# Last neighbourhood group of each layer: low parts of stored rows on GpSimd, gate parts over three steps, output matmuls placed anew

## Chip, cores and metric

One core of one Trainium2 chip. The metric is the device time of one execution in microseconds, lower is better; several executions were timed, and one more was profiled.

## The reference

Two layers of a bidirectional encoder over 1024 positions of width 1024, all in float32, then a last RMS norm:

```python
def hybrid_layer(x, g, w_in, w_out, ...):
    h = rms_norm(x, g)
    z = einsum('bsd,de->bse', h, w_in)
    qd, kd, vd, qn, kn, vn, gate = split(z)
    o_da = diff_attention(qd, kd, vd, lam, lam_init, subln_g)     # 4 heads of 2 x 64, full attention
    o_na = neighbourhood_attention(qn, kn, vn, rpb)               # 8 heads of 64, 8 rows x 16 columns around a position
    o = concatenate([o_da, o_na], axis=-1) * silu(gate)
    return x + einsum('bse,ed->bsd', o, w_out)
```

## The kernel before

Everything is kept transposed: a row block of 128 features by 1024 positions. A float32 product is made of three matmuls in a rounded format (`three`, L930 to L934): high by high, low by high, high by low, where the high part is a rounded copy and the low part the difference to the original. So each operand of a matmul is first copied by ScalarE (ACT; the high part) and then subtracted by VectorE (DVE) or GpSimd (POOL; the low part). A **part** in this text is the three 128x512 matmuls of one k, one of eight row blocks of `h`; a **piece** is the eight parts that give 128 output features for one half (512 positions). The seven first rows of an output piece can be summed early; its last one comes from the last group.

A layer has eight head groups, four of differential attention and four of neighbourhood attention (two heads each). Each runs in steps 1 to 8, one tile of 128 queries a step (`steps`, `step` at L1138): TensorE (PE) makes the scores of the next tile, transposes the probabilities of the last one in blocks of four (`turn_p`), each block copied to `pt_hi` by ACT (L772) and subtracted to `pt_lo` by DVE (L1364), and in even steps weighs the values with a pair of tiles (L1077, L1078) after transposing the reciprocals of the softmax sums (L1088). DVE adds the bias and takes the maximum (L1356), ACT takes the exponential (L797), and `output_pair` (L1410 to L1414) brings a pair into `gate`. Between these blocks, in slots 0 to 3 of `fill`, TensorE does the projection of the group that comes next: V, K, Q and gate pieces, one piece a step, eight parts each. So there is always a step's worth of projection to cover the softmax chain.

The last group of a layer has no next group. Its gate pieces are projected in step 8 of the group before (half 0) and in its own step 1 (half 1), in step 2 there are no parts, and from step 3 on the slots hold parts of the output projection (`LAST_FILL`, `out_piece`). The gated results of the first seven groups wait in DRAM (`mixed_dram`). They are loaded as rows into `h_lo` (L518) as soon as the last piece of `h` has used that row (`row_freed`, counted by the parts of gate half 1), copied to `h_hi` by ACT (`take_mixed`, L831) and subtracted in place by DVE (L1438), at the steps in `TAKEN`. Output parts of pieces 0 and 1 wait for the row of their k (`h_ready`). The weights come in chunks of two pieces: DMA into `w_raw` (L483), high part by ACT (L730), low part by POOL (L577); output chunks 1 to 4 are made at the steps in `LAST_CHUNKS`. POOL also finishes the gate (`silu`, L607 and L609: after ACT's tanh, L757) and spreads the reciprocals (`widen`, L621).

Every engine runs its own queue in the order of the program; the tables say in which step and slot something stands:

```python
    LAST_CHUNKS = {2: 1, 6: 2, 7: 3, 8: 4}
    TAKEN = {2: [0, 1], 3: [2, 3], 4: [4, 5], 5: [6]}
    both = lambda ks: [(t, [k]) for k in ks for t in (0, 1)]
    LAST_FILL = {1: [], 2: [], 3: [[], both([0]), both([1])], 4: [both([2]), [], both([3])],
```

An entry `(p, ks)` stands for the parts `ks` of output piece `p`; the lists of a step are its slots.

Of the kernel before, what the change touches and what calls it, by code (L numbers as in the profile page):

```python
# [26 lines left out]
def hybrid_encoder(nc, x_t, chunks, norm_gain, final_gain, subln_gain, lam_vecs, bias_rows, out_t):  # L27
    D, S = x_t.shape
    NT = D // P
# [31 lines left out]
    LAST_CHUNKS = {2: 1, 6: 2, 7: 3, 8: 4}  # L61
    TAKEN = {2: [0, 1], 3: [2, 3], 4: [4, 5], 5: [6]}
# [131 lines left out]
    with ExitStack() as ctx:  # L194
# [216 lines left out]
        def groups(e, l, attend):  # L411
# [136 lines left out]
        def _(pool):  # L548
# [45 lines left out]

            def mask_edge(l, i):
# [37 lines left out]
            def attend(g, behind):  # L633
                for t, front, ft in steps(g, behind):
                    if front and front.projects(ft) and ft % 2 == 0:
                        w_lo_part(front.chunk(ft) + 1, 1 - front.buffer(ft))
                    if t == 1:
                        silu(g, 0)
                    if front and front.na and t < NT:
                        widen(front, ft)  # L640
                    if t == 1:
                        silu(g, 1)
# [10 lines left out]
                    if not behind and t in LAST_CHUNKS:  # L653
                        out_lo_part(g.l, LAST_CHUNKS[t])
# [39 lines left out]
        def _(act):  # L694
# [144 lines left out]
            def attend(g, behind):  # L839
                for t, front, ft in steps(g, behind):  # L840
# [6 lines left out]
                    if not g.na and t % 2 and t >= 3:  # L847
                        mean_square(g, (t - 3) // 2)
                    for c in range(2):
# [7 lines left out]
                    if front and front.projects(ft) and ft:  # L857
                        piece_part(front, ft)
                    taken = [] if behind else TAKEN.get(t, [])
                    for i in taken[:1]:  # L860
                        take_mixed(g.l, i)
                    if t % 2 == 0:
                        output_half(g, t - 1)
                    if t == NT and behind:
# [4 lines left out]
                        piece_part(behind, 0)  # L869
# [3 lines left out]
                    for i in taken[1:]:  # L873
                        take_mixed(g.l, i)
# [52 lines left out]
        def _(pe):  # L927
# [186 lines left out]
            def step(g, behind, t, front, ft, ended=None):  # L1114
# [8 lines left out]

                def fill(j):
# [3 lines left out]
                    if front and front.projects(ft):  # L1128
# [128 lines left out]
        def _(dve):  # L1257
# [178 lines left out]
            def take_mixed(l, i):  # L1436
                dve.wait_ge(h_hi_done, l * (2 * NT + 1) + NT + i + 1)
# [135 lines left out]
```

## Time and profile before

| what | us |
|---|---|
| median of three runs | 1508.54 |
| the three runs | 1502.69 to 1509.71 |
| the profiled execution | 1503.38 |
| its span | 1501.6 |
| TensorE busy | 1437.1 |
| VectorE busy | 895.6 |
| ScalarE busy | 684.9 |
| GpSimd busy | 459.4 |

The span lies within the execution's own time; all times in rows are counted from the span's start. Layer 0's last group runs from 609.5 to some 690 us, layer 1's from 1340.9 to some 1420 us. Busy time says how long an engine worked, not who waited for whom; for that the rows name the releaser of an idle time in square brackets.

### The profile page before, as it was taken

The numbers are of one execution on the slowest core, as the hardware profiler recorded it, in microseconds if no ns is written. First come the engines' busy times: TensorE is split into PE (matmuls) and PEld (weight loads), VectorE is DVE, ScalarE is ACT, GpSimd is POOL, SyncE is SP. The second block draws the span as 40 slices with busy tenths as digits, with TensorE's granted clock in tenths as the row PEclk, the third lists the DMA queues.
The fourth block names the chain that finished last, engine by engine and source line by source line (L and its number), as shares of the span: only waits on it lengthen the run. The fifth ranks groups of instructions, "written<-read, shape, count | busy, mean of one in ns | idle before, by whom it ended". The sixth has DMA issues, their size and how long they took to land.

```text
span 1501.6 us, 24043 instructions
## 1 busy us (share of the span) xinstructions
PE 1437.1 (96%) x8160; PEld 1170.8 (78%) x8160; DVE 895.6 (60%) x1828; ACT 684.9 (46%) x1306; POOL 459.4 (31%) x370
## 2 busy tenths in 40 slices
PE   7999999999999999899999999999999999997994
PEld 6788787878787888677887878787788888876874
DVE  6666666767655555653436667766666555557323
ACT  5445455544444444542524544544544444445330
POOL 2322223223323232313633132312322323331261
PEclk9999999999999999999999999999999999999997
DMA  4700101021111110301110001010102111121012
GB/s 175 147 29 28 43 21 49 21 60 36 45 51 55 40 59 35 133 15 57 56 47 37 24 35 35 30 40 21 53 22 74 43 52 42 52 96 58 29 56 112
DMA packets 39246, 79.41 MB, mean 53 GB/s; under 512 B 18832, under 2 KB 18832, under 8 KB 39184
## 3 DMA queue, kind: packets, MB, share of 16 engines
q1 hardware_dynamic: 39184, 78.60, 15.7%
q8 instruction: 37, 0.61, 0.2%
q14 instruction: 25, 0.20, 0.0%
HBM read 66.57 MB, written 15.96 MB: 55 GB/s over the span
## 4 chain that ended last, share of the span: by engine, by line
PE 87%; DVE 4%; issue 3%; ACT 2%; SPq 2%; DMA 1%; POOL 0%; DVEq 0%; POOLq 0%; ACTq 0%
PE proj L932 18%; PE proj L934 17%; PE proj L933 17%; PE scores L968 9%; PE turn L1025 5%; PE mix L1077 3%; PE mix L1078 3%; PE mix L1042 2%; PE mix L1041 2%; PE mix L1043 2%; SPq L476 2%; PE scores L1025 2%; DVE prob L1356 1%; PE mix L1051 1%; ACT prob L797 1%
## 5 line engine op out<-in xcount | busy, mean ns | idle before, releaser
L932 PE MATMUL proj<-h_hi,w_hi 128*128 128x512 f32 x1184 | 501.2, 423 | 18.3 <-DVE h_lo L1265 10.1
L934 PE MATMUL proj<-h_hi,w_lo 128*128 128x512 f32 x1184 | 467.3, 395 | 0.0
L933 PE MATMUL proj<-h_lo,w_hi 128*128 128x512 f32 x1184 | 464.3, 392 | 0.0
L932 PEld LDWEIGHTS proj<-h_hi,w_hi 128*128 128x128 f32 x1184 | 223.4, 189 | 82.9 <-issue 36.0
L934 PEld LDWEIGHTS proj<-h_hi,w_lo 128*128 128x128 f32 x1184 | 223.1, 188 | 51.6
L933 PEld LDWEIGHTS proj<-h_lo,w_hi 128*128 128x128 f32 x1184 | 224.5, 190 | 34.3
L1356 DVE CUSTOM_DVE_ANT_0 prob<-scores,inner 128x1024 f32<-128x1024 f32 (+1 forms) x192 | 204.0, 1062 | 72.1 <-PE scores L968 71.4
L577 POOL TENSOR_TENSOR w_lo<-w_raw,w_hi 128x1024 fp32r<-128x1024 f32 x78 | 191.8, 2459 | 179.5 <-ACT w_hi L730 179.4
L1364 DVE TENSOR_TENSOR pt_lo<-turn,pt_hi 128x512 fp32r<-128x512 f32 x208 | 139.2, 669 | 152.5 <-ACT pt_hi L772 151.2
L772 ACT ACTIVATE pt_hi<-turn 128x512 fp32r<-128x512 f32 x208 | 120.5, 579 | 224.4 <-PE turn L1025 223.6
L797 ACT ACTIVATE prob<-prob,nm,escale_now 128x1024 f32<-128x1024 f32 x128 | 158.0, 1235 | 3.3 <-DVE nm L1360 3.2
L1025 PE MATMUL turn<-ident,prob 128*128 128x128 f32 x768 | 116.3, 274 | 16.0 <-DVE pt_lo L1364 11.4
L1025 PEld LDWEIGHTS turn<-ident,prob 128*128 128x128 f32 x768 | 93.3, 140 | 47.4 <-DVE pt_lo L1364 17.3
L621 POOL COPY rrec_wide<-rrec 128x128 f32<-128x128 f32 x64 | 18.6, 291 | 300.1 <-DVE rrec L1389 215.9
L968 PE MATMUL scores<-k_hi,q_hi 64*128 64x512 f32 (+1 forms) x448 | 106.7, 432 | 0.0
L730 ACT ACTIVATE w_hi<-w_raw 128x1024 fp32r<-128x1024 f32 x78 | 82.2, 1054 | 39.0 <-DMA w_raw<-chunks 14.5
L797 ACT ACTIVATE prob<-prob,nm 128x576 f32<-128x576 f32 (+1 forms) x128 | 95.0, 742 | 8.9 <-DVE nm L1360 8.9
L968 PE MATMUL scores<-k_hi,q_lo 64*128 64x512 f32 (+1 forms) x448 | 95.8, 377 | 0.0
L968 PE MATMUL scores<-k_lo,q_hi 64*128 64x512 f32 (+1 forms) x448 | 95.5, 375 | 0.0
L592 POOL TENSOR_TENSOR q_lo<-q_next,q_hi 128x512 fp32r<-128x512 f32 x32 | 41.4, 1293 | 149.6 <-ACT q_hi L762 149.6
L607 POOL TENSOR_SCALAR gate_tanh<-gate_tanh 128x512 f32<-128x512 f32 x32 | 47.8, 1493 | 127.8 <-ACT gate_tanh L757 127.2
L628 POOL TENSOR_TENSOR rms<-msq,power 128x2 f32<-128x2 f32 x32 | 22.6, 705 | 205.0 <-ACT msq L824 205.0
(162 smaller groups left out, 2248.8 us busy)
## 6 DMA issues: line engine op xcount, KB each, us to landing
w_raw<-chunks SPq DMA_DIRECT2D x81, 512.0 KB, 3.2
mixed_dram<-gate SPq DMA_DIRECT2D x28, 256.0 KB, 2.0
edge<-bias_dram SPq DMA_DIRECT2D x32, 224.0 KB, 3.8
h_lo<-mixed_dram SPq DMA_DIRECT2D x14, 512.0 KB, 7.5
xt<-x_t SPq DMA_DIRECT2D x8, 512.0 KB, 9.1
bias_dram<-bias_rows SPq DMA_DIRECT2D x16, 240.0 KB, 5.8
out_t<-prob SPq DMA_DIRECT2D x6, 512.0 KB, 3.0
out_t<-gate SPq DMA_DIRECT2D x2, 512.0 KB, 3.0
```

The costliest lines, as they stand in the source:

```text
L577: pool.tensor_tensor(w_lo[:, b], w_raw[:], f32(w_hi[:, b]), ALU.subtract).then_inc(w_lo_done, 1)
L607: pool.tensor_scalar(gate_tanh[:], gate_tanh[:], 1.0, None, ALU.add).then_inc(gate_plus, 1)
L730: act.activation(w_hi[:, b], w_raw[:], ACT.Copy).then_inc(w_hi_done, 1)
L772: act.activation(dst, src, ACT.Copy).then_inc(turn_hi, 1)
L797: act.activation(s, s, ACT.Exp, bias=nm[:, b, m:m + 1], scale=scale, accum_out=rsum[:, b, m:m + 1]).then_inc(exp_done, 1)
L932: pe.matmul(dst, a_hi, b_hi, start=start, stop=False)
L933: pe.matmul(dst, a_hi, b_lo, start=False, stop=False)
L934: return pe.matmul(dst, a_lo, b_hi, start=False, stop=stop)
L968: return pe.matmul(out, (q_hi, q_lo, q_hi)[p][own, tile], (k_hi, k_hi, k_lo)[p][own, cols], start=p == 0, stop=p == 2)
L1025: last = pe.transpose(dst[:, k * P:(k + 1) * P], prob_of(g.na, t, m, first + k * P, first + (k + 1) * P), ident[:])
L1356: dve.tensor_tensor_reduce(prob_of(g.na, t, m, 0, w), all_scores[:, at:at + w], bias, 1.0, -3e38, ALU.add, ALU.max, mx[:, b, m:m + 1]).the ...
L1364: dve.tensor_tensor(dst, src, f32(hi), ALU.subtract).then_inc(turn_freed, 1)
```

## The change

The low parts of the seven stored rows go from VectorE (`take_mixed`, L1438) to GpSimd (`row_lo`). ScalarE's high parts of these rows stand at new places (`ROWS_HI`: three lists a step, behind the first block of probabilities, ahead of and behind the copy of the mixed pair), GpSimd's in `ROWS_LO`. The sixteen gate parts of the last group, before eight in step 8 of the group before and eight in step 1, become four in that step 8 (`GATE_HEAD`), eight in step 1 and four in step 2 (`GATE_FILL`), and the work on a gate half (scaling, tanh, silu) follows one step later, GpSimd's half 1 in step 3 behind rows 2 and 3. The output parts: steps 3 and 4 as before, step 5 gets two more and step 6 one, steps 7 and 8 two and one fewer; output chunk 1 moves from step 2 to step 4 on ScalarE and GpSimd, there behind rows 4 to 6. The group before the last is written out behind its loop.

```diff
-    LAST_CHUNKS = {2: 1, 6: 2, 7: 3, 8: 4}
-    TAKEN = {2: [0, 1], 3: [2, 3], 4: [4, 5], 5: [6]}
+    LAST_CHUNKS = {4: 1, 6: 2, 7: 3, 8: 4}
+    ROWS_HI = {2: ([0], [1], [2]), 3: ([3], [], []), 4: ([4], [5], [6])}
+    ROWS_LO = {2: [0, 1], 3: [2, 3], 4: [4, 5, 6]}
+    GATE_HEAD = [range(0, 1), range(1, 2), range(2, 4)]
+    GATE_FILL = {1: [[(0, range(4, 6))], [(0, range(6, 8)), (1, range(0, 1))], [(1, range(1, 4))]],
+                 2: [[], [(1, range(4, 6))], [(1, range(6, 8))]]}
...
-                 5: [both([4]), [], both([5])], 6: [both([6]), [(2, range(0, 3))], [(2, range(3, 7))]],
-                 7: [[(3, range(0, 3))], [(3, range(3, 7)), (4, range(0, 2))], [(4, range(2, 7))]],
-                 8: [[(5, range(0, 4))], [(5, range(4, 7))], [(6, most)], [(7, most)]]}
+                 5: [both([4]), both([5]), both([6])],
+                 6: [[(2, range(0, 3))], [(2, range(3, 6))], [(2, range(6, 7)), (3, range(0, 3))]],
+                 7: [[(3, range(3, 6))], [(3, range(6, 7)), (4, range(0, 3))], [(4, range(3, 7)), (5, range(0, 1))]],
+                 8: [[(5, range(1, 4))], [(5, range(4, 7))], [(6, most)], [(7, most)]]}
...
-            with e.Fori(0, NA_G - 1) as i:
+            last = Group(l, True, NA_G - 1, project=False)
+            with e.Fori(0, NA_G - 2) as i:
                 attend(Group(l, True, i), Group(l, True, i + 1))
-            attend(Group(l, True, NA_G - 1, project=False), None)
+            attend(Group(l, True, NA_G - 2), last)
+            attend(last, None)
...
+            def row_lo(l, i):
+                pool.wait_ge(h_hi_done, l * (2 * NT + 1) + NT + i + 1)
+                pool.tensor_tensor(h_lo[:, i, :], f32(h_lo[:, i, :]), f32(h_hi[:, i, :]), ALU.subtract)\
+                    .then_inc(h_ready, 1)
...
-                    if t == 1:
+                    if t == 1 and g.project:
                         silu(g, 0)
+                    for i in ROWS_LO[t] if not behind and t in ROWS_LO else []:
+                        row_lo(g.l, i)
+                    if not behind and t in LAST_CHUNKS:
+                        out_lo_part(g.l, LAST_CHUNKS[t])
                     if front and front.na and t < NT:
                         widen(front, ft)
                     if t == 1:
+                        silu(g, 1 if g.project else 0)
+                    if t == 3 and not g.project:
                         silu(g, 1)
...
                     for c in range(2):
                         p_part(g, t - 1, c)
+                        for i in rows[0] if c == 0 else []:
+                            take_mixed(g.l, i)
                         if front:
                             exponentials(front, ft, c)
...
-            def take_mixed(l, i):
-                dve.wait_ge(h_hi_done, l * (2 * NT + 1) + NT + i + 1)
-                dve.tensor_tensor(h_lo[:, i, :], f32(h_lo[:, i, :]), f32(h_hi[:, i, :]), ALU.subtract)\
-                    .then_inc(h_ready, 1)
```

TensorE's order in step 2 of the last group. `scores` is both the score tile and one of two banks that transposed blocks go to; `turn` is the other. Before:

```order
L968 MATMUL scores<-k_lo,q_hi 128x512 x2
L1025 MATMUL turn<-ident,prob 128x128 x4
L1025 MATMUL scores<-ident,prob 128x128 x4
L1088 MATMUL turn<-ident,rrec_wide 128x128 x2
L1077 MATMUL mix<-pt_hi,v_hl 128x256
```

and of the changed kernel:

```order
L992 MATMUL scores<-k_lo,q_hi 128x512 x2
L1049 MATMUL turn<-ident,prob 128x128 x4
L956 MATMUL proj<-h_hi,w_hi 128x512
L957 MATMUL proj<-h_lo,w_hi 128x512
L958 MATMUL proj<-h_hi,w_lo 128x512
L956 MATMUL proj<-h_hi,w_hi 128x512
L957 MATMUL proj<-h_lo,w_hi 128x512
L958 MATMUL proj<-h_hi,w_lo 128x512
L1049 MATMUL scores<-ident,prob 128x128 x4
```

Two gate parts now stand between the two transposed blocks, and two more behind the second.

GpSimd's queue from the first gate half of the last group to output chunk 1 (`w_lo<-w_raw,w_hi`), before:

```order
L607 TENSOR_SCALAR gate_tanh<-gate_tanh 128x512
L609 TENSOR_TENSOR gate<-gate,gate_tanh 128x512
L621 COPY rrec_wide<-rrec 128x128
L607 TENSOR_SCALAR gate_tanh<-gate_tanh 128x512
L609 TENSOR_TENSOR gate<-gate,gate_tanh 128x512
L621 COPY rrec_wide<-rrec 128x128
L577 TENSOR_TENSOR w_lo<-w_raw,w_hi 128x1024
```

and of the changed kernel:

```order
L621 TENSOR_SCALAR gate_tanh<-gate_tanh 128x512
L623 TENSOR_TENSOR gate<-gate,gate_tanh 128x512
L606 TENSOR_TENSOR h_lo<-h_lo,h_hi 128x1024 x2
L635 COPY rrec_wide<-rrec 128x128
L606 TENSOR_TENSOR h_lo<-h_lo,h_hi 128x1024 x2
L635 COPY rrec_wide<-rrec 128x128
L621 TENSOR_SCALAR gate_tanh<-gate_tanh 128x512
L623 TENSOR_TENSOR gate<-gate,gate_tanh 128x512
L606 TENSOR_TENSOR h_lo<-h_lo,h_hi 128x1024 x3
L586 TENSOR_TENSOR w_lo<-w_raw,w_hi 128x1024
```

Seven subtractions of rows now stand ahead of the chunk, four of them ahead of the second gate half.

ScalarE's queue in steps 2 and 3 (`pt_hi` is a high part of probabilities, `h_hi` of a stored row, `u<-mix` the mixed pair), before:

```order
L772 ACTIVATE pt_hi<-turn 128x4x128
L797 ACTIVATE prob,rsum<-prob,nm 128x512
L772 ACTIVATE pt_hi<-scores 128x4x128
L797 ACTIVATE prob,rsum<-prob,nm 128x512
L831 ACTIVATE h_hi<-h_lo 128x1024
L812 ACTIVATE u<-mix 64x256
L813 ACTIVATE u<-mix 64x256
L730 ACTIVATE w_hi<-w_raw 128x1024
L831 ACTIVATE h_hi<-h_lo 128x1024
```

and of the changed kernel:

```order
L790 ACTIVATE pt_hi<-turn 128x4x128
L849 ACTIVATE h_hi<-h_lo 128x1024
L815 ACTIVATE prob,rsum<-prob,nm 128x512
L790 ACTIVATE pt_hi<-scores 128x4x128
L815 ACTIVATE prob,rsum<-prob,nm 128x512
L775 ACTIVATE gate_tanh<-gate 128x512
L849 ACTIVATE h_hi<-h_lo 128x1024
L830 ACTIVATE u<-mix 64x256
L831 ACTIVATE u<-mix 64x256
L849 ACTIVATE h_hi<-h_lo 128x1024
```

Row 0 now stands between the two blocks of probabilities, rows 1 and 2 around the mixed pair, and chunk 1 has left.

## Rows read from the trace of the kernel before

**Rows 1.** the page's busy time of each engine, us, share of the span, instructions.

```profile
PE 1437.1 (96%) x8160; PEld 1170.8 (78%) x8160; DVE 895.6 (60%) x1828; ACT 684.9 (46%) x1306; POOL 459.4 (31%) x370
```

**Rows 2.** TensorE's losing stretch of both layers, busy us and instructions.

```profile
core 0: us, PE busy (x) PEld busy (x) DVE busy (x) ACT busy (x) POOL busy (x), PEclk, DMA share, GB/s
617.03:654.89 37.86, 28.88 (x166) 22.71 (x165) 29.83 (x64) 21.02 (x39) 6.38 (x8) 0.91 0.21 85
1348.43:1386.61 38.18, 28.89 (x166) 22.49 (x165) 29.84 (x64) 21.30 (x40) 6.38 (x8) 0.91 0.23 90
```

**Rows 3.** TensorE in order of time, layer 0: start us, us, operation [idle before <-releaser].

```profile
598.78 0.50 PE L932 MATMUL proj<-h_hi,w_hi 128*128 128x512 f32 x1
...
609.50 0.50 PE L968 MATMUL scores<-k_hi,q_hi 64*128 64x512 f32 x2
...
610.40 0.50 PE L932 MATMUL proj<-h_hi,w_hi 128*128 128x512 f32 x1
...
617.03 0.51 PE L968 MATMUL scores<-k_hi,q_hi 64*128 64x512 f32 x2
...
617.94 0.66 PE L1025 MATMUL turn<-ident,prob 128*128 128x128 f32 x4
618.43 0.60 PE L1025 MATMUL scores<-ident,prob 128*128 128x128 f32 x4
...
621.70 0.69 PE L1088 MATMUL turn<-ident,rrec_wide 128*128 128x128 f32 x2 [2.67 <-DVE pt_lo L1364]
...
625.61 0.50 PE L968 MATMUL scores<-k_hi,q_hi 64*128 64x512 f32 x2
...
631.19 0.50 PE L932 MATMUL proj<-h_hi,w_hi 128*128 128x512 f32 x1 [2.20 <-DVE h_lo L1438]
...
633.57 0.81 PE L968 MATMUL scores<-k_hi,q_hi 64*128 64x64 f32 x2
...
641.16 0.39 PE L1077 MATMUL mix<-pt_hi,v_hl 128*128 128x256 f32 x1 [0.67 <-DVE pt_lo L1364]
...
643.27 0.51 PE L968 MATMUL scores<-k_hi,q_hi 64*128 64x64 f32 x2
...
649.13 0.44 PE L1021 MATMUL turn<-ident,prob 128*128 128x128 f32 x2 [2.09 <-DVE pt_lo L1364]
...
650.89 0.51 PE L968 MATMUL scores<-k_hi,q_hi 64*128 64x64 f32 x2
...
654.89 0.50 PE L932 MATMUL proj<-h_hi,w_hi 128*128 128x512 f32 x1 [0.49 <-DVE xt L1489]
```

**Rows 4.** the tile h_lo: min/median/max ns, first and last start.

```profile
L831 ACT ACTIVATE h_hi<-h_lo x14: 1041/1048/1062, 622.2 to 1380.4; 128x1024 fp32r<-128x1024 f32 x14
L1438 DVE TENSOR_TENSOR h_lo<-h_lo,h_hi x14: 1218/1224/2593, 623.3 to 1381.5; 128x1024 fp32r<-128x1024 f32 x14
...
DMA to landing us min/median/max: 3.6/7.5/8.9
```

**Rows 5.** VectorE in order of time, layer 0, steps 2 and 3.

```profile
627.40 0.42 DVE L1414 TENSOR_TENSOR gate<-u,gate 128x256 f32<-128x256 f32 x1
628.55 2.59 DVE L1438 TENSOR_TENSOR h_lo<-h_lo,h_hi 128x1024 fp32r<-128x1024 f32 x1 [0.72 <-ACT h_hi L831]
```

**Rows 6.** GpSimd in order of time, layer 0, output chunk 1.

```profile
627.64 2.41 POOL L577 TENSOR_TENSOR w_lo<-w_raw,w_hi 128x1024 fp32r<-128x1024 f32 x1 [4.68 <-ACT w_hi L730]
```

**Rows 7.** groups: line, engine, names, shapes, count | busy us, mean ns | idle before.

```profile
L1364 DVE TENSOR_TENSOR pt_lo<-turn,pt_hi 128x512 fp32r<-128x512 f32 x208 | 139.2, 669 | 152.5 <-ACT pt_hi L772 151.2
...
L772 ACT ACTIVATE pt_hi<-turn 128x512 fp32r<-128x512 f32 x208 | 120.5, 579 | 224.4 <-PE turn L1025 223.6
...
L577 POOL TENSOR_TENSOR w_lo<-w_raw,w_hi 128x1024 fp32r<-128x1024 f32 x78 | 191.8, 2459 | 179.5 <-ACT w_hi L730 179.4
...
L607 POOL TENSOR_SCALAR gate_tanh<-gate_tanh 128x512 f32<-128x512 f32 x32 | 47.8, 1493 | 127.8 <-ACT gate_tanh L757 127.2 <-issue 0.4
L609 POOL TENSOR_TENSOR gate<-gate,gate_tanh 128x512 f32<-128x512 f32 x32 | 41.1, 1286 | 2.7
```

More of the change, by code:

```diff
@@ L652, in attend @@
                         widen(front, ft, g)
-                    if not behind and t in LAST_CHUNKS:
-                        out_lo_part(g.l, LAST_CHUNKS[t])
             def norm_stats(n):
@@ L848, in attend @@
                         mean_square(g, (t - 3) // 2)
+                    rows = ROWS_HI[t] if not behind and t in ROWS_HI else [[]] * 3
                     for c in range(2):
                         p_part(g, t - 1, c)
+                        for i in rows[0] if c == 0 else []:
+                            take_mixed(g.l, i)
                         if front:
@@ L856, in attend @@
                         sum_squared(front, ft)
-                    if front and front.projects(ft) and ft:
+                    if not g.project:
+                        if t in GATE_FILL:
+                            piece_part(g, t - 1)
+                    elif front and front.projects(ft) and ft:
                         piece_part(front, ft)
-                    taken = [] if behind else TAKEN.get(t, [])
-                    for i in taken[:1]:
+                    for i in rows[1]:
                         take_mixed(g.l, i)
@@ L863, in attend @@
                         output_half(g, t - 1)
+                    for i in rows[2]:
+                        take_mixed(g.l, i)
                     if t == NT and behind:
@@ L868, in attend @@
                             mean_square(g, PAIRS - 1)
-                        piece_part(behind, 0)
+                        if behind.project:
+                            piece_part(behind, 0)
                     if not behind:
@@ L872, in attend @@
                             out_hi_part(g.l, LAST_CHUNKS[t])
-                    for i in taken[1:]:
-                        take_mixed(g.l, i)
             def out_hi_part(l, j):
@@ L1122, in step @@
                     sum_pair(g, (t - 3) // 2)
+                if t == NT and behind and not behind.project:
+                    parts = GATE_HEAD
                 def fill(j):
@@ L1127, in fill @@
                             out_piece(g.l, p, ks)
-                    if front and front.projects(ft):
+                    if not g.project:
+                        for p, ks in GATE_FILL[t][j] if t in GATE_FILL else []:
+                            group_piece(g, p, ks)
+                    elif front and front.projects(ft):
                         group_piece(front, ft, parts[j])
@@ L1463, in step @@
                     combine(front, ft)
-                if front and front.projects(ft) and ft:
+                if not g.project:
+                    if t in GATE_FILL:
+                        piece_part(g, t - 1)
+                elif front and front.projects(ft) and ft:
                     piece_part(front, ft)
                 add_pieces(2)
-                taken = [] if behind else TAKEN.get(t, [])
-                for i in taken[:1]:
-                    take_mixed(g.l, i)
                 if g.na and t % 2 == 0:
@@ L1478, in step @@
                         v_part(behind, c)
-                    piece_part(behind, 0)
-                for i in taken[1:]:
-                    take_mixed(g.l, i)
+                    if behind.project:
+                        piece_part(behind, 0)
                 if t == NT and not g.na and behind.na:
@@ L1514, in _ @@
                 from_second(dve, l, step)
+                dve.wait_ge(h_ready, l * HR + NT + NT - 1)
                 for hf in range(2):
```

## The prediction

> **What bounds the kernel now.** I read the page's busy times first, then the stages, then TensorE's rows of the last neighbourhood group, and last the rows of the engines that it waits for. TensorE is busy 96% of the span [rows 1], so only its gaps and slow stretches can be won back. The stage view shows where they are: in the 37.9 us from step 2 of the last group to the first matmul of output piece 2 (layer 0), TensorE is busy 28.9 us and its granted clock is 0.91; the same stretch of layer 1 takes 38.2 us with 28.9 [rows 2]. VectorE is busy 29.8 us there, more than TensorE, GpSimd only 6.4.
>
> [rows 3] give the steps. A score block costs 0.9 us (609.50 to 610.40), a transpose block 0.45 to 0.5 (617.94 to 618.43), the weighing of an outer pair 2.1 (641.16 to 643.27); eight parts (a part is the three matmuls of one k) and two transpose blocks take 6.6 (610.40 to 617.03), so a part is 0.70. Against that, the steps 2 to 5 last 8.6, 8.0, 9.7 and 7.6 us, while their work is 3.9 (0.9 + 2x0.45 + 2.1), 4.6 (0.9 + 0.9 + 4x0.70), 7.0 and 5.1 us: 13.3 us lost per layer, and 0.5 more before 654.89. The gaps named are 2.67, 2.20, 0.67, 2.09 and 0.49 us, all ended by VectorE. Much of the rest is clock: the score matmul at 633.57 lasts 0.81 us, the same one at 643.27 lasts 0.51 [rows 3]; the granted clock of 0.91 says that for about a fifth of the stretch the level was 1.2 GHz in place of 2.4, here 2 us behind the gap of 2.20.
>
> VectorE is late for two reasons. In steps 2 to 5 it makes the low parts of seven stored rows at 1.22 us each and up to two a step, in line with the softmax [rows 4]. And one of them, at 628.55, takes 2.59 us [rows 5]: it starts while GpSimd's subtraction of 627.64 runs [rows 6], and ends 1.1 us after that does, as if it had been held until 630.05.
>
> **What the change does, part by part.** The 56 output parts and 16 gate parts stay; no matmul is added.
>
> *Gate parts.* Four of the sixteen leave step 8 of the group before; step 1 keeps eight; step 2, which has none, gets four. Step 8 shrinks by 4x0.70 = 2.8. Its weighing then needs the last low probability tile earlier, which comes by way of ACT (0.58) and VectorE (0.67) [rows 7]; between no wait and 2.8 I take 1.0, since today's order shows no gap but little room. So step 2 starts 1.8 to 2.0 earlier, at 615.0 instead of 617.03 [rows 3]. Its work is 3.9 + 2.8 = 6.7: the 2.67 us gap is filled.
>
> *Output parts.* Piece 0 and 1 still start in step 3, but are complete at the end of step 5, which gets two parts more (5.1 + 1.4 = 6.5). From the first part of piece 2 on, both kernels have the same 42 output parts left. That gives one mark to compare: today it falls at 654.89 less one transpose block, 654.4.
>
> *Low parts.* Seven leave VectorE, 7x1.22 = 8.5 us per layer. On GpSimd I price one at 2.40 to 2.46, the same subtraction of the same size [rows 6, 7]. The row first: 2.41 against 1.22 us, a factor of two. The Trainium skill (GPSIMD Engine Reference, Engine selection) says the same of two-input elementwise work, and by its table would leave it on VectorE. By its figure alone 7 ops would cost 8.5 us more of engine time; whether that costs anything depends on who waits.
>
> GpSimd's queue from step 1, in layer 0's clock: gate half 0 comes to it about 615.8 and takes 1.49 + 1.29 [rows 7], to 618.7. Row 0 to 621.1. ACT reaches row 1 only behind the second tanh, at about 622.5, so rows 1, 2 and 3 end at 624.9, 627.7 and 630.2 (with a short copy between), gate half 1 at 633.4, rows 4 to 6 at 635.8, 638.2, 640.6 and output chunk 1, moved from step 2 to step 4 and behind them, at 643.0. Stored row 0 is freed at 612.5, and must land before 616.9; the shortest landing is 3.6, the median 7.5 us [rows 4]; the first of the batch should be the short one. At 7.5, ACT's queue is held for some 3 us in step 2, and with it the last tile of that step; at the median it would cost up to 3 us per layer.
>
> *The walk on TensorE.* Step 2: 615.0 + 6.7 + 0.3 wait = 622.0. Step 3: 4.6, and 0.4 since VectorE's gate product (0.42 us, two SBUF inputs like the row of 628.55 [rows 5]) can be held by GpSimd's row 1: 627.0. Step 4: 7.0, and 1.75 because ACT copies row 4 (1.05 [rows 4]) and an exponential ahead of the tile that the weighing needs: 635.75. Step 5: 6.5 and 0.45 for a tile behind that gate product: 642.7. Score block 1.25: piece 2 starts at 643.95, against 654.4. Gain 10.5 per layer. If the gate product of step 4 also loses its place to row 6, VectorE is 2.4 late and piece 2 starts at 646.1: gain 8.3. The middle is 9.4; for a fall of the clock in one layer of three (about 1.3 us each, 3 us of work at half rate) I take off 0.4. So 9 us per layer, 18 in all. Behind the mark I take 0: chunks 2 to 4 keep their steps; piece 4, the first on chunk 2, now starts three parts (2.1 us) earlier within step 7, which bounds a loss there.
>
> *The rest.* One more group body written out of the loop (in each layer the loop runs 2 times, not 3): today's written-out last group loses no time at its start, 609.50 to 617.03; I take 0, with 1 us per layer as the upper end. The wait of VectorE before the last row's low part comes long after the seven: 0.
>
> Profiled execution: 1503.38 - 18 = 1485.4. The three runs shown lie at 1502.69 to 1509.71, the profiled one near their low end; the mean of the four is 1506.1. Against that I give **1488 us**.
>
> **The rivals.**
> (a) *No waits left.* If all 2.8 us of step 8 count and no step waits, piece 2 starts at 640.1: 14.3 per layer, 1477 us. Against it: ACT's order in step 4.
> (b) *The chain stays.* If steps 2 to 5 are long because of score, softmax, exponential, transpose in series and not because of the rows, they keep their 7.6 to 8.6 us, and only the moved parts count: 1.8 + 1.4 = 3.2 per layer, 6.4 in all, about 1499. For it: three of the gaps are ended by the low probability tile, not by a row. Against it: the step just ahead, from 598.78 to 609.50, has the same series and eight parts, and no gap [rows 3].
> (c) *Slower: GpSimd becomes the bound through the shared SBUF port.* From 622.5 on its chain holds seven subtractions and 3.5 us of other work, so chunk 1 is ready at 626 + 7x for a subtraction of x us. At 2.4 that is 642.8, just before it is wanted; at 4.06 it is today's 654.4, and beyond that the kernel is slower. If each subtraction were held by VectorE as VectorE's was, twice its length, 4.8, the mark would be 659.6: 5.2 per layer, 1516 us. For it: the pair at 627.64 and 628.55 shows that one engine holds the other. The Trainium skill (GPSIMD Engine Reference, Key points) says the two share their SBUF interfaces and contend when a VectorE instruction has two SBUF inputs; by it alone this could go either way. Against: in the same pair GpSimd's 2.41 is not stretched, its mean over 78 is 2.46 [rows 7], and VectorE keeps few instructions with two SBUF inputs here once the rows have left.
> (d) *GpSimd late by part of that*, x between 3.5 and 4.06, or the stored rows landing late on top of (b): within 0.5%.
>
> **How the numbers follow.** The walk 0.68, (a) 0.07, (b) 0.14, (c) 0.06, (d) 0.05. The walk's own range is 1480 to 1496: 8.3 to 10.5 per layer, less up to 3 for the landing, over run levels of 1503 to 1509. With (a) below and (b) above, 1478 to 1500 leaves out some 0.15. A measurement here tells about 0.5% from no change, 7.5 us, so 1501 and under is faster: nearly all of the walk, (a), and part of (b), 0.80; same 0.14; slower 0.06.
>
> **What would show it.** Right: piece 2's first matmul at 643 to 647 in layer 0; no gap of 2 us or more in steps 2 to 5; granted clock near 1.0 between the marks; low parts of rows on GpSimd at 2.4 us; one VectorE gate product of 0.42 us stretched by 0.5 to 2.4. Wrong: gaps on TensorE ended by GpSimd's low row or chunk 1 (c); gaps as large as now, ended by the low probability tile (b); ACT idle for DMA in step 2 (late landing); the subtractions on GpSimd well over 2.6 us.

## The result, and the profile of the changed kernel

| | before | changed |
|---|---|---|
| median of four runs, us | 1508.59 | 1486.88 |
| the four runs, us | 1502.69 to 1509.71 | 1484.41 to 1487.66 |
| the profiled execution, us | 1503.38 | 1487.66 |
| its span, us | 1501.6 | 1485.9 |

The ratio of the times is 0.9858 (95% interval 0.9837 to 0.9878): the changed kernel is faster by 1.4%, 21.7 us between the medians and 15.7 between the two profiled executions. The prediction said faster, at 1488.0 us.

First the page's busy times of the changed kernel, to be read against [rows 1]:

```profile
PE 1434.3 (97%) x8160; PEld 1168.9 (79%) x8160; DVE 877.3 (59%) x1814; ACT 684.4 (46%) x1306; POOL 492.0 (33%) x384
```

TensorE runs the same 8160 matmuls in 2.8 us less. VectorE has fourteen instructions fewer, GpSimd fourteen more: the rows of two layers. GpSimd's 32.6 us are 2.33 for each, VectorE's 18.3 are 1.31.

The stage view from step 2 of the last group to the first matmul of output piece 2, in both layers, columns as in [rows 2]:

```profile
core 0: us, PE busy (x) PEld busy (x) DVE busy (x) ACT busy (x) POOL busy (x), PEclk, DMA share, GB/s
616.36:647.23 30.87, 28.89 (x174) 23.37 (x173) 19.32 (x52) 21.12 (x39) 25.70 (x17) 0.94 0.34 128
1339.69:1370.50 30.81, 28.96 (x181) 23.48 (x180) 21.00 (x56) 21.12 (x39) 25.73 (x17) 1.00 0.38 140
```

Here the gain can be seen whole. TensorE is as busy as before, 28.9 us, but in 30.9 us in place of 37.9 and 38.2. (The four gate parts of step 2 now stand in it, 2.8 us; before, about as much went in slow matmuls.) VectorE is down from 29.8 to 19.3 and 21.0, GpSimd up from 6.4 to 25.7, its fullest stretch. The granted clock is 1.00 in layer 1, and 0.94 in layer 0, for a reason that the next rows show: TensorE in order of time, layer 0, columns as in [rows 3].

```profile
616.36 0.50 PE L992 MATMUL scores<-k_hi,q_hi 64*128 64x512 f32 x2
...
621.52 0.38 PE L1101 MATMUL mix<-pt_hi,v_hl 128*128 128x256 f32 x1 [0.18 <-DVE pt_lo L1394]
...
623.62 0.50 PE L992 MATMUL scores<-k_hi,q_hi 64*128 64x512 f32 x2
...
628.32 0.51 PE L992 MATMUL scores<-k_hi,q_hi 64*128 64x64 f32 x2
...
635.58 0.39 PE L1101 MATMUL mix<-pt_hi,v_hl 128*128 128x256 f32 x1 [1.75 <-DVE pt_lo L1394]
...
637.14 0.41 PE L1101 MATMUL mix<-pt_hi,v_hl 128*128 128x256 f32 x1
...
638.55 0.81 PE L992 MATMUL scores<-k_hi,q_hi 64*128 64x64 f32 x2
...
645.88 0.51 PE L992 MATMUL scores<-k_hi,q_hi 64*128 64x64 f32 x2
...
647.23 0.50 PE L956 MATMUL proj<-h_hi,w_hi 128*128 128x512 f32 x1
```

Of the gaps of 2.67, 2.20, 0.67, 2.09 and 0.49 us in [rows 3] only the third stands, the one before the weighing of step 4, and it has grown from 0.67 to 1.75. Behind it, in this layer, the matmuls of the weighing slow from 0.28 to 0.41 us and the next score matmul lasts 0.81: for some 3 us the granted clock was at 1.2 in place of 2.4 GHz.

The rows on ScalarE and GpSimd (the tile `h_lo`, columns as in [rows 4]), and GpSimd's queue in layer 0 in order of time:

```profile
L849 ACT ACTIVATE h_hi<-h_lo x14: 1041/1052/1062, 618.5 to 1361.6; 128x1024 fp32r<-128x1024 f32 x14
L606 POOL TENSOR_TENSOR h_lo<-h_lo,h_hi x14: 2360/2396/2453, 620.3 to 1362.8; 128x1024 fp32r<-128x1024 f32 x14
...
DMA to landing us min/median/max: 3.2/6.9/8.0
```

```profile
620.26 2.39 POOL L606 TENSOR_TENSOR h_lo<-h_lo,h_hi 128x1024 fp32r<-128x1024 f32 x1
623.93 2.40 POOL L606 TENSOR_TENSOR h_lo<-h_lo,h_hi 128x1024 fp32r<-128x1024 f32 x1 [1.28 <-ACT h_hi L849]
...
626.73 4.76 POOL L606 TENSOR_TENSOR h_lo<-h_lo,h_hi 128x1024 fp32r<-128x1024 f32 x2
...
634.49 4.71 POOL L606 TENSOR_TENSOR h_lo<-h_lo,h_hi 128x1024 fp32r<-128x1024 f32 x2
640.59 2.45 POOL L606 TENSOR_TENSOR h_lo<-h_lo,h_hi 128x1024 fp32r<-128x1024 f32 x1 [1.39 <-ACT h_hi L849]
643.00 2.39 POOL L586 TENSOR_TENSOR w_lo<-w_raw,w_hi 128x1024 fp32r<-128x1024 f32 x1
```

No subtraction is stretched: 2.36 to 2.45 us, the price taken from [rows 6, 7]. GpSimd is busy 25.7 of these 30.9 us, but TensorE never waits for it there.

The same 30 us cost VectorE one stretched product. VectorE in order of time, layer 0:

```profile
625.57 1.04 DVE L1444 TENSOR_TENSOR gate<-u,gate 128x256 f32<-128x256 f32 x1
...
640.35 0.42 DVE L1444 TENSOR_TENSOR gate<-u,gate 128x256 f32<-128x256 f32 x1
```

The first starts inside GpSimd's subtraction of row 1 (623.93 + 2.40 = 626.33) and ends 0.28 us after it: it was held. The second starts 0.24 us ahead of row 6 and isn't. Layer 1 has the same pair (1.04 and 0.42).

**Where the 15.7 us come from.** I cut each trace at the first transposes of V of every group, which both kernels have at the same places; us between these marks, the two layers beside each other, and the time in which TensorE sat idle with a named releaser in the 60 us behind the mark of the last group:

| trace | start of the run | groups before step 8 | step 8 | last group and output | idle of that | span |
|---|---|---|---|---|---|---|
| before | 52.8 | 482.2, 480.8 | 73.5, 73.5 | 177.1, 161.7 | 8.9, 9.3 | 1501.6 |
| before, second | 53.9 | 481.5, 481.3 | 73.5, 73.5 | 178.8, 164.0 | 10.5, 10.2 | 1506.4 |
| changed | 53.6 | 482.9, 481.2 | 71.4, 71.3 | 170.8, 154.7 | 1.9, 1.8 | 1485.9 |
| changed, second | 53.3 | 482.2, 481.0 | 71.3, 71.4 | 169.2, 154.5 | 1.9, 1.8 | 1482.9 |
| rows_only | 53.4 | 482.1, 480.9 | 73.5, 73.5 | 177.5, 161.9 | 9.9, 9.8 | 1502.7 |
| rows_chunk4 | 53.1 | 481.0, 480.7 | 73.5, 73.5 | 176.0, 161.7 | 8.7, 8.8 | 1499.3 |
| low_on_dve | 51.9 | 482.0, 481.1 | 71.4, 71.4 | 179.0, 163.1 | 6.5, 6.4 | 1499.8 |
| pool_doubled | 52.5 | 481.5, 481.0 | 71.4, 71.4 | 182.0, 167.2 | 10.7, 8.4 | 1506.9 |
| old_fill | 51.7 | 481.2, 481.0 | 71.4, 71.4 | 171.1, 156.9 | 3.6, 3.9 | 1484.6 |

("Step 8" is the interval between two marks that contains it. The traces come from single executions: low_on_dve's is the slowest of its six, rows_chunk4's the fastest of its twelve.) In the profiled pair, step 8 gives 2.1 in each layer and the last group with the output 6.3 and 7.0: 17.6 us. The start of the run and the six earlier groups of each layer take 1.9 back, and hold nothing that the change touches in substance: over all traces the start scatters from 51.5 to 54.0, the groups from 480.7 to 482.9. Of the 17.6, 14.5 are idle time gone (18.2 less 3.7); the other 3.1 agree with the 2.8 that TensorE's busy time fell by.

### The profile page after: what moved, and what is told of

It is laid out like the page before. It is cut to its first block, busy times and chain, and to the rows that moved or that the text cites. A ratio compares the mean times of both kernels' runs of the same rounds, so it can differ in the third digit from the quotient of the medians.

```text
span 1485.9 us, 23642 instructions
## 1 busy us (share of the span) xinstructions
PE 1434.3 (97%) x8160; PEld 1168.9 (79%) x8160; DVE 877.3 (59%) x1814; ACT 684.4 (46%) x1306; POOL 492.0 (33%) x384
## 4 chain that ended last, share of the span: by engine, by line
PE 89%; DVE 3%; ACT 2%; issue 2%; SPq 2%; DMA 1%; POOL 0%; DVEq 0%; POOLq 0%; ACTq 0%
PE proj L956 19%; PE proj L958 17%; PE proj L957 17%; PE scores L992 10%; PE turn L1049 5%; PE mix L1101 3%; PE mix L1102 3%; PE mix L1066 2%; PE mix L1065 2%; PE mix L1067 2%; PE scores L1049 2%; SPq L485 2%; PE mix L1075 1%; ACT prob L815 1%; DVE pt_lo L1394 1%
## 5 line engine op out<-in xcount | busy, mean ns | idle before, releaser
L1049 PEld LDWEIGHTS turn<-ident,prob 128*128 128x128 f32 x768 | 93.2, 140 | 47.8 <-DVE pt_lo L1394 17.6
L790 ACT ACTIVATE pt_hi<-scores 128x512 fp32r<-128x512 f32 (+1 forms) x80 | 44.1, 552 | 89.2 <-PE scores L1049 89.2
```

What stands on the lines that cost most here:

```text
L790: act.activation(dst, src, ACT.Copy).then_inc(turn_hi, 1)
L1049: last = pe.transpose(dst[:, k * P:(k + 1) * P], prob_of(g.na, t, m, first + k * P, first + (k + 1) * P), ident[:])
```

## The experiments

Each kernel was run beside the kernel before on the same chip; ratios are to it. The kernel before had medians of 1507.49 (17 runs), 1507.51 (27) and 1505.49 (7) us in the three sets, so the 1503.38 of its profiled execution is at the low end.

### The two kernels again

The kernel before, unchanged. Its first runs had lain in two lots, at 1502.7 to 1503.4 and near 1509.

> The kernel before, unchanged, profiled again. Its timed runs lie at two levels, 1502.7 to 1503.4 and 1508.5 to 1509.7 us; the profile shown was one of the lower. If this one is at the higher level, theory A (the extra 5 to 6 us are more stretches of TensorE's clock at its lower level behind the gaps of the last groups) expects the stretch from step 2 to the first part of piece 2 at 40 us or more with a granted clock under 0.91; theory B (they lie elsewhere, in the start, the end or loads) expects that stretch at 37.9 and 38.2 us and a difference in other places.

Measured: 1508.18 us, span 1506.4. The waits of TensorE from 595 to 662 us, and the stage view over the stretches of [rows 2]:

```profile
PE proj L932 <- DVE h_lo L1438: 4.3, 2, 2.3
PE turn L1088 <- DVE pt_lo L1364: 2.7, 1, 2.7
PE turn L1021 <- DVE pt_lo L1364: 2.1, 1, 2.1
```

```profile
617.34:656.85 39.51, 28.93 (x165) 22.86 (x164) 29.82 (x64) 21.01 (x39) 6.38 (x8) 0.91 0.22 84
1350.89:1391.51 40.62, 30.47 (x166) 23.93 (x165) 29.84 (x64) 21.29 (x40) 6.39 (x8) 0.87 0.21 83
```

The same program is 1.7 and 2.4 us longer in the two stretches, and 0.8 us elsewhere (the table). In layer 0 it is the wait for the second row, 2.28 us at 636.82 in place of 0.74; in layer 1 the same wait (0.9 us more idle time in all) and more slow clock, 0.87 (busy 30.5 us in place of 28.9). So most of the difference between these two traces of the kernel before is made in the stretch that the change mends: where gaps and slow clock fall differs from run to run. Theory A held in part: layer 0 came out at 39.5 us and a clock of 0.91, against 40 or more and under 0.91. And there are no two lots: of the 51 executions of the kernel before that were timed beside the experiments, one took 1501.30 us, and the others fill the range from 1503.41 to 1510.43 with no gap of 1 us.

The changed kernel, unchanged:

> The changed kernel, unchanged, timed beside the runs of the kernel before on the same chip: 1485 to 1488 us, ratio 0.984 to 0.988. Theory A (clock) expects its runs closer together than those of the kernel before, since no gap of over 2 us is left.

Measured: 1485.12 us, five runs within 1484.7 to 1485.57, ratio 0.985 (0.9837 to 0.9862), against 1504.11 to 1510.43 for the 17 runs beside it. The last groups have the same gaps as in the first profile (1.9 and 1.8 us), no slow clock behind the 1.75, and are 1.5 us shorter in layer 0. With the gaps of 2 us and more, the scatter has gone.

### One part of the change at a time

**rows_only**: the kernel before, with the low parts of the seven rows on GpSimd at the steps in which VectorE made them. Gate parts, output parts and ScalarE's order stay.

```diff
-                dve.tensor_tensor(h_lo[:, i, :], f32(h_lo[:, i, :]), f32(h_hi[:, i, :]), ALU.subtract)\
+                pool.tensor_tensor(h_lo[:, i, :], f32(h_lo[:, i, :]), f32(h_hi[:, i, :]), ALU.subtract)\
...
+                    for i in taken[:1]:
+                        row_lo(g.l, i)
                     if not behind and t in LAST_CHUNKS:
                         out_lo_part(g.l, LAST_CHUNKS[t])
+                    for i in taken[1:]:
+                        row_lo(g.l, i)
```

> The kernel before with one part of the change: the seven low parts per layer go from VectorE to GpSimd, at the same steps; gate parts, output parts, chunk 1 and ScalarE's order stay. My theory (both parts are needed; the rows are worth about half): in steps 3 to 5 the gaps ended by h_lo on VectorE go, but the row is ready 1.2 us later on GpSimd, and step 2 keeps its gap of some 2.7 us; 4 to 6 us less than before in all, 1500 to 1503. Rival (the rows alone are the cause): 12 us or more less. Rival (GpSimd's twofold length eats it): no gain, TensorE's gaps now ended by POOL h_lo.

Measured: 1504.76 us (12 runs), ratio 0.9989 (0.9978 to 1.0). That is less than the 1500 to 1503 expected, and near the last rival: the part of the change that the profile of before seems to ask for, VectorE's relief, brings 0.1%. TensorE in order of time, layer 0:

```profile
622.16 0.49 PE L1098 MATMUL turn<-ident,rrec_wide 128*128 128x128 f32 x2 [2.67 <-DVE pt_lo L1374]
...
633.09 0.80 PE L942 MATMUL proj<-h_hi,w_hi 128*128 128x512 f32 x1 [3.47 <-POOL h_lo L597]
...
653.93 0.50 PE L942 MATMUL proj<-h_hi,w_hi 128*128 128x512 f32 x1 [1.85 <-POOL h_lo L597]
```

The gap of 2.67 us in step 2 stays to the hundredth: it never was the rows' doing, step 2 had nothing to run. And the waits for rows are now for GpSimd's. Row 1 comes behind chunk 1 in GpSimd's queue:

```profile
628.29 2.43 POOL L577 TENSOR_TENSOR w_lo<-w_raw,w_hi 128x1024 fp32r<-128x1024 f32 x1 [2.14 <-ACT w_hi L740]
630.67 2.36 POOL L597 TENSOR_TENSOR h_lo<-h_lo,h_hi 128x1024 fp32r<-128x1024 f32 x1
```

It is ready at 633.0, and TensorE starts at 633.09, after 3.47 us. So is the queue order the culprit?

**rows_chunk4**: rows_only, with chunk 1 at step 4. It stands behind row 4 there, but ahead of row 5; in the changed kernel it stands behind rows 4 to 6.

```diff
-    LAST_CHUNKS = {2: 1, 6: 2, 7: 3, 8: 4}
+    LAST_CHUNKS = {4: 1, 6: 2, 7: 3, 8: 4}
```

> As rows_only, but with output chunk 1 at step 4 as in the changed kernel, so that GpSimd's row 1 doesn't stand behind it. rows_only gained 2.7 us only; its largest gap, 3.5 us, was ended by POOL h_lo, and that row stood behind chunk 1. If the queue was the cause, that gap goes and the gain is 6 to 9 us (1499 to 1502); the 2.7 us gap of step 2 stays. If the rows on GpSimd are worth nothing by themselves, it stays at 1504 to 1507.

Measured: 1503.79 us (12 runs), ratio 0.9985 (0.9974 to 0.9995), less than expected. The wait of 3.47 us is gone, and three take its place; TensorE, layer 0:

```profile
629.30 0.50 PE L942 MATMUL proj<-h_hi,w_hi 128*128 128x512 f32 x1 [0.99 <-POOL h_lo L597]
633.42 0.50 PE L942 MATMUL proj<-h_hi,w_hi 128*128 128x512 f32 x1 [1.24 <-POOL h_lo L597]
...
647.16 0.50 PE L942 MATMUL proj<-h_hi,w_hi 128*128 128x512 f32 x1 [1.50 <-POOL h_lo L597]
```

The first two are about what a subtraction takes more on GpSimd (2.4 against 1.22 us): row 1 and row 2 are needed as soon as before, and come later. The third is the queue again. GpSimd, layer 0:

```profile
642.37 2.43 POOL L577 TENSOR_TENSOR w_lo<-w_raw,w_hi 128x1024 fp32r<-128x1024 f32 x1 [0.75 <-ACT w_hi L740]
644.76 2.35 POOL L597 TENSOR_TENSOR h_lo<-h_lo,h_hi 128x1024 fp32r<-128x1024 f32 x1
```

Row 5 stands behind chunk 1 and is ready at 647.11. So chunk 1 was moved from one row to another, and rows alone with the chunk clear of all rows was not tried. By these rows such a kernel could save some 1.5 us per layer of TensorE's idle time, an estimate; the gap of 2.67 us in step 2 is there in this kernel too.

**low_on_dve**: the other half, the changed kernel with the seven low parts back on VectorE at the old steps.

```diff
-    ROWS_LO = {2: [0, 1], 3: [2, 3], 4: [4, 5, 6]}
+    TAKEN = {2: [0, 1], 3: [2, 3], 4: [4, 5], 5: [6]}
...
+                taken = [] if behind else TAKEN.get(t, [])
+                for i in taken[:1]:
+                    take_mixed(g.l, i)
                 add_pieces(2)
...
+                for i in taken[1:]:
+                    take_mixed(g.l, i)
```

> The changed kernel with its low parts of stored rows back on VectorE (steps 2 to 5, two a step, the last ahead of the additions in step 5); gate parts over three steps and output parts as changed. My theory: the moved gate parts keep step 8 (2.1 us per layer) and fill the gap of step 2, but VectorE stays the bound in steps 3 to 5: 10 to 13 us less than before, 1493 to 1497. Rival (placement is everything): within 2 us of the changed kernel. Rival (rows are everything): 3 us or less under the kernel before.

Measured: 1497.6 us (6 runs, 1493.03 to 1501.9), ratio 0.9925 (0.9908 to 0.9943). TensorE, layer 0:

```profile
628.92 0.50 PE L949 MATMUL proj<-h_hi,w_hi 128*128 128x512 f32 x1 [1.40 <-DVE h_lo L1461]
...
634.95 0.39 PE L1094 MATMUL mix<-pt_hi,v_hl 128*128 128x256 f32 x1 [1.75 <-DVE pt_lo L1387]
...
645.98 0.79 PE L949 MATMUL proj<-h_hi,w_hi 128*128 128x512 f32 x1 [2.63 <-DVE h_lo L1461]
```

The gap of step 2 is gone with the gate parts in it; the gaps ended by VectorE's rows stay, and behind 2.63 us the matmuls are slow (0.79 us in place of 0.50). Against the runs beside them, rows alone bring 2 to 3 us, placement alone about 10, both about 22: more than the sum. But row 6 is at a bad place in this kernel. Its part stands in step 5, where the changed kernel has it (before: step 6), and VectorE makes the row late in that step, from 644.72, though its high part was ready at 639.0. So a part of the 2.63 us may be of this order and not of VectorE as such.

Could VectorE do the seven rows at a better place? **low_on_dve_early** has row 6 in step 4 too:

```diff
-    TAKEN = {2: [0, 1], 3: [2, 3], 4: [4, 5], 5: [6]}
+    TAKEN = {2: [0, 1], 3: [2, 3], 4: [4, 5, 6]}
```

> As low_on_dve, but all rows as early as ScalarE gives them (2, 2 and 3 in steps 2 to 4), so that row 6 isn't late by its place. low_on_dve gave 1497.6 and 10 us under the kernel before, with 4.2 us of gaps per layer ended by VectorE's rows, 2.6 of them by row 6 in step 5. If its place was the cause of that, this one gains 3 to 5 us on low_on_dve (1493); if VectorE's load is the cause, the gap moves to step 4 and the time stays at 1497. It should not reach the changed kernel (1485 to 1487) in either case, unless GpSimd is no part of the gain.

Measured: 1503.46 us (10 runs: nine from 1497.84 to 1505.53, and one of 3591.54 that is not in the ratio and has no explanation here), ratio 0.9966 (0.9953 to 0.998), worse than expected: the gap of 2.63 has moved to the next tile in line. TensorE, then VectorE and GpSimd, layer 0:

```profile
649.33 0.69 PE L1038 MATMUL turn<-ident,prob 128*128 128x128 f32 x2 [3.69 <-DVE pt_lo L1387]
```

```profile
642.28 4.55 DVE L1461 TENSOR_TENSOR h_lo<-h_lo,h_hi 128x1024 fp32r<-128x1024 f32 x2
```

```profile
643.13 2.62 POOL L586 TENSOR_TENSOR w_lo<-w_raw,w_hi 128x1024 fp32r<-128x1024 f32 x1 [8.82 <-ACT w_hi L741]
```

Rows 5 and 6 take VectorE 4.55 us in place of 2.44: row 6 starts inside GpSimd's subtraction of chunk 1, which ends at 645.75, and lasts 3.41 us, until 646.83. So some 2.1 of the 3.69 us are one engine held by the other, and the run does not tell VectorE's load from the place of its rows. An order of VectorE's rows clear of chunk 1 and ahead of the tiles of step 5 was not tried, and might come nearer to the changed kernel than 1497.6. Shown is that the changed kernel is 12.5 us faster than the better of the two orders tried.

### How dear may GpSimd be?

**pool_doubled**: the changed kernel, each row's subtraction followed by a product with one, which leaves the values as they are.

```diff
+                    sub.then_inc(doubled, 1)
+                    pool.wait_ge(doubled, l * len(DOUBLED) + DOUBLED.index(i) + 1)
+                    sub = pool.tensor_tensor(h_lo[:, i, :], f32(h_lo[:, i, :]), ones[:].to_broadcast([P, S]), ALU.mult)
```

> The changed kernel with each of GpSimd's seven row subtractions followed by a second operation of the same size on the same tile (times one), so that a row takes about 4.8 us in place of 2.4. The prediction's rival (c) in numbers: GpSimd's chain ends 14 us later per layer (six doubled rows behind row 0, and 1 us of row 0), the mark at the first part of piece 2 moves by the same, with gaps on TensorE ended by POOL h_lo and POOL w_lo, and the whole takes 1485 + 28 = 1513 us, more than the kernel before. If less than 8 us are lost, GpSimd had slack that the walk didn't see.

Measured: 1507.41 us (10 runs), ratio 1.0003 (0.9993 to 1.0012): the whole gain is lost, 22.3 us against the second run of the changed kernel. GpSimd and then TensorE, layer 0:

```profile
617.76 2.40 POOL L608 TENSOR_TENSOR h_lo<-h_lo,h_hi 128x1024 fp32r<-128x1024 f32 x1
620.24 1.90 POOL L612 TENSOR_TENSOR h_lo<-h_lo,ones 128x1024 fp32r<-128x1024 f32 x1
...
651.52 2.37 POOL L588 TENSOR_TENSOR w_lo<-w_raw,w_hi 128x1024 fp32r<-128x1024 f32 x1
```

```profile
626.58 0.50 PE L962 MATMUL proj<-h_hi,w_hi 128*128 128x512 f32 x1 [2.08 <-POOL h_lo L612]
...
647.31 0.50 PE L962 MATMUL proj<-h_hi,w_hi 128*128 128x512 f32 x1 [2.41 <-POOL h_lo L612]
651.62 0.51 PE L962 MATMUL proj<-h_hi,w_hi 128*128 128x512 f32 x1 [1.99 <-POOL h_lo L612]
```

A row costs 2.4 + 1.9 = 4.3 us here, not the 4.8 that I had expected. At that price the changed kernel equals the kernel before; the prediction had put this point at 4.06 in rival (c).

### The wait that is left, and the output parts

The gap of 1.75 us comes from ScalarE's order: row 4 is copied ahead of the tile. **row4_later** moves that copy behind it:

```diff
-    ROWS_HI = {2: ([0], [1], [2]), 3: ([3], [], []), 4: ([4], [5], [6])}
+    ROWS_HI = {2: ([0], [1], [2]), 3: ([3], [], []), 4: ([], [4, 5], [6])}
```

> The changed kernel with ScalarE's high part of row 4 moved behind the second exponential of step 4, beside row 5. In the changed kernel the largest gap left on TensorE is 1.75 us ahead of the weighing of step 4, in the profile of both its runs; my walk blamed ScalarE's row 4 (1.05 us) standing ahead of the tile. If so, that gap falls to 0.7 us and each layer gains 1.0, 2 us in all, perhaps 1 or 2 more where the clock no longer falls behind the gap: 1482 to 1484 against 1485 to 1487. Rival: GpSimd then gets row 4 late and the gap comes back in step 5, ended by POOL h_lo: same time.

Measured: 1485.0 us, ratio 0.9858 (0.9841 to 0.9875), the same as the changed kernel (1485.12 and 1486.88). The gap before the weighing falls to 0.80 us, and this comes up, VectorE and then GpSimd in layer 0:

```profile
636.01 2.12 DVE L1444 TENSOR_TENSOR gate<-u,gate 128x256 f32<-128x256 f32 x1
```

```profile
633.10 7.28 POOL L606 TENSOR_TENSOR h_lo<-h_lo,h_hi 128x1024 fp32r<-128x1024 f32 x3 [1.11 <-ACT h_hi L849]
```

The three subtractions now run without a break, the product starts inside the second and is held until it ends, at 637.84 by that instruction's own record (the product's own end is 638.13). Its lateness, and a row that is 0.3 us late, cost the next step what the weighing gained (gaps of 0.27 and 0.64 us; against the changed kernel's second trace step 4 is 0.9 us shorter and step 5 1.5 longer).

**pair_late** is meant to keep VectorE's products away from the path: the mixed pair of steps 2, 4 and 6 is brought into the gate one step later. **row4_pair_late** has both edits.

```diff
+                if not g.project and t in (3, 5, 7):
+                    output_pair(g, t - 2)
...
-                    output_pair(g, t - 1)
+                    if g.project or t == NT:
+                        output_pair(g, t - 1)
```

> The changed kernel; in the last group VectorE brings in the mixed pair of steps 2, 4 and 6 one step later, behind the probabilities, so that its gate product (two SBUF inputs, held for 0.6 us by GpSimd's row 1 in step 2) no longer stands ahead of the next tile's scores. Theory (the hold costs TensorE what it costs VectorE): 0.4 us per layer at step 4's score block, 1 us in all, 1484. Rival: the product is only held elsewhere and holds the reciprocals: no difference.

> row4_later with the same move. There the gap ahead of the weighing of step 4 fell from 1.75 to 0.80 us, but the whole gained nothing; in its trace the gate product of step 4 lasts 2.12 us in place of 0.42, since it meets GpSimd's row 4, and 1.0 us of gaps appears in step 5. If that hold is why, this kernel gains the lost 1 us per layer back: 1482 to 1483, the fastest so far. If step 5's gaps have another cause, it stays at 1485.

Measured: 1487.6 us, ratio 0.9875 (0.9855 to 0.9894), and 1486.68, 0.9874 (0.9855 to 0.9893). The kernel before had 1505.49 us beside these two and old_fill, so their ratios say more than their times. The gap before the weighing shrinks to 1.00 and 0.2 us, but the sum of an output piece (`xt`) now stands behind the products, and TensorE waits 1.42 and 1.11 us for it. The rival's hold came too: at its new place the first product takes 1.7 us. No version beats the changed kernel; of the 1.9 us idle a layer in it, row4_later has as much at other places, the other two 2.4 to 3.3.

**old_fill**: the changed kernel with the output parts of steps 5 to 8 placed as before.

```diff
-                 5: [both([4]), both([5]), both([6])],
+                 5: [both([4]), [], both([5])], 6: [both([6]), [(2, range(0, 3))], [(2, range(3, 7))]],
```

> The changed kernel with the output parts of steps 5 to 8 where they were (piece 0 and 1 complete in step 6). The walk says that step 5 then lasts as long as its softmax chain, with a gap of 1 to 2 us where two parts stood, and that these 1.4 us of work come later: 1 to 1.4 us per layer, 1487 to 1488 in place of 1485. Rival: the parts only wait for their rows in step 5 and gain nothing there: same time.

Measured: 1487.78 us, ratio 0.9884 (0.9864 to 0.9904). By the marks the last group and the output take 1.1 and 2.3 us longer than the mean of the changed kernel's two traces (170.0 and 154.6), as expected. TensorE's waits in layer 0 (us, times, longest), where the changed kernel has 1.9 and 0.3:

```profile
PE mix L1100 <- DVE pt_lo L1393: 1.9, 2, 1.7
PE turn L1044 <- DVE pt_lo L1393: 1.4, 2, 1.0
PE proj L955 <- DVE xt L1512: 0.7, 1, 0.7
```

The first wait is the changed kernel's; the other two are back in steps 5 and 6, whose slots have two parts and one fewer.

## Why the prediction was right

The time (1488.0 against 1486.88), the sign and the mechanism held, and so did most of the terms. That the time came within 1.1 us is in part luck: the prediction took 1506.1 us for the kernel before, 2.5 under its median, and 18 us for the gain, 3.7 under the one measured, and the two partly cancel. Its range, 1480 to 1496, lies 2 us lower at both ends than its own parts give (1503 - 21 = 1482 and 1509 - 10.6 = 1498); the measured time lies in both. One by one:

- **Step 8 and the start of step 2.** Predicted 1.8 to 2.0 us earlier, by way of 2.8 less a wait of 1.0. Measured 2.1 in each layer, in every kernel that has the new gate parts.
- **The walk.** Lengths of the steps in layer 0, us:

| step | predicted | changed | changed, second |
|---|---|---|---|
| 2 | 7.0 | 7.26 | 7.26 |
| 3 | 5.0 | 4.70 | 4.69 |
| 4 | 8.75 | 10.23 | 9.37 |
| 5 | 6.95 | 7.33 | 6.68 |
| to piece 2 | 1.25 | 1.35 | 1.36 |

- **The mark.** Predicted 8.3 to 10.5 us earlier in a layer, in the middle 9.4. The first traces of both kernels have piece 2 at 654.4 and 647.23. The changed one comes to its last-but-one group 1.45 us later (start and earlier groups), so it gains 8.6; the second trace has piece 2 at 644.71, 0.45 us late by the same count, and gains 10.1. Both are against the first, faster trace of the kernel before.
- **The gaps.** No gap of 2 us is left; the gap of 1.75 us in step 4 came out as it was priced. Step 4 was still 0.6 us longer than the walk in the trace without slow clock. Its rows say why: the two transposes of the reciprocals take 0.44 us and stand in no term of the walk, and the four parts take 3.06 us in place of 2.80, less 0.1 on the transposes of probabilities.
- **GpSimd.** The queue walk had row 0 end at 621.1 and chunk 1 ready at 643.0; measured 622.65 and 645.39, of which 1.45 is the later run. The last 1 us is row 6: ScalarE copies it at 639.45, behind the mixed pair, and GpSimd waits 1.39 us for that. It cost nothing, since piece 2 started at 647.23.
- **The hold.** Predicted: 0.4 us for the gate product behind row 1, and a chance that the one of step 4 goes behind row 6. Measured: 1.04 for 0.42 in step 3, for which TensorE did not wait: the step took 4.70 and not 5.0, so this 0.4 was no term of TensorE's. At the second place the product wins by 0.24 us. row4_later shows the other outcome, 2.12 us.
- **The landing.** I kept up to 3 us open for stored row 0. ScalarE copies it at 618.50, directly behind the block before it: nothing was waited for.
- **The clock.** I took 0.4 us a layer, for one fall in three layers at 1.3 us. The one fall seen cost 1.5 us (steps 4 and 5 in the two traces: 17.56 and 16.05) and lasted some 3 us. So 1.3 was a fair price, but not for "3 us of work at half rate", which would take 3 us more; it fits 3 us of elapsed time. Of the twelve last groups in the six kernels and repeats that have rows on GpSimd at 2.4 us and gate parts in step 2, one shows a granted clock under 1.00. In those with gaps of 2 us or more (the kernel before, rows_only, rows_chunk4, low_on_dve and its variant, pool_doubled) every last group does: 0.90 to 0.97 in the 50 us from 610 or 1335. One in three was too many.
- **The two levels.** Later runs show one range and no two levels. The prediction put the profiled execution at 1485.4, 18 us less, and it came out at 1487.66: the layers gave 17.6, the start and earlier groups took 1.9. Between the medians the gain is 21.7 us, since the profiled execution of before is a low one; before_again shows where a usual one loses 4 us more.

The rivals: (a), no waits left, 1477, was not reached, for the reason given against it. (b), only the moved parts count, 1499, lies near low_on_dve's 1497.6, but its mechanism, steps that stay at 7.6 to 8.6 us whatever becomes of the rows, did not show: the changed kernel's steps 3 and 5 take 4.7 and 6.7 to 7.3 us. (c) was a matter of price: break-even forecast at 4.06 us a subtraction, measured near 4.3, and the real price 2.40. Its mechanism showed a little otherwise: TensorE waits for the rows (9.6 us in six waits in layer 0), not for the chunk.

What the prediction did not see is how the two halves depend on each other. It booked the low parts as 8.5 us of VectorE's time per layer and the gate parts as 2.8 us of cover, as if each had its own share. Rows on GpSimd come 1.2 us later each and need the cover that the moved parts give; the moved parts didn't close the gaps in the two orders in which VectorE kept the rows. On TensorE's idle time in a layer (before 9.7 by the mean of four) rows alone leave 9.9 and 9.8, placement alone 6.5 and 6.4, both 1.9 and 1.8.

Still open: how near VectorE could come with its rows in a better order; whether the loop's written-out body costs anything under 1 us (no kernel kept the loop; the earlier groups show no step); and what GpSimd's rows would do if they landed late, which no run had.

## What to carry to other kernels

When an engine that others wait for is relieved by a slower one, ask for each moved piece who needs its result and when: at twice the time it must start earlier or be needed later, and here it was the moved cover that paid for that, and the relief alone brought 0.1%. Gaps on TensorE cost more than their length, since here the granted clock fell behind those of about 2 us; count them together. And look at what stands in the helper's queue ahead of the moved work, and at which two-input instructions of the relieved engine will start inside it.

## What the runs showed of the hardware

- **One engine holds the other, both ways.** A VectorE instruction with two inputs in SBUF that starts while GpSimd subtracts waits until that ends: 0.42 became 1.04, 1.69 (pool_doubled) and 2.12 us, 1.22 became 2.59 and 3.41. GpSimd is held as well, where VectorE came first. In low_on_dve VectorE's two rows run from 627.66 to 630.09, and GpSimd's copy and scaling take 1.11 and 2.45 us in place of 0.29 and 1.49:

```profile
627.66 2.43 DVE L1461 TENSOR_TENSOR h_lo<-h_lo,h_hi 128x1024 fp32r<-128x1024 f32 x2
```

```profile
627.91 1.11 POOL L630 COPY rrec_wide<-rrec 128x128 f32<-128x128 f32 x1 [8.33 <-DVE rrec L1412]
628.99 2.45 POOL L616 TENSOR_SCALAR gate_tanh<-gate_tanh 128x512 f32<-128x512 f32 x1
```

The longer length is a wait and not a slower pace: each ends within its own usual time, some 0.14 us less, behind the other engine's end. `pt_lo`, whose one input is in PSUM, keeps its 0.68 to 0.69 us beside GpSimd's subtractions throughout. The Trainium skill (GPSIMD Engine Reference, Key points) says that the two engines share their SBUF interfaces and contend where a VectorE instruction has two SBUF inputs; both halves agree with these rows, and the length of the wait is the traces' own.
- **The price on GpSimd.** 2.40 us against 1.22 for 128x1024 with two full inputs; with a single column spread over the row as the second input (pool_doubled) it took 1.89 to 1.96.
- **The scatter of a kernel can be a symptom.** The kernel before spread over 1501.3 to 1510.4 us, the changed one over 1484.4 to 1487.7. In the two traces of each, most of the difference arises in the stretch from step 2 to piece 2.
